# HGRN's tile products in seven visits a group instead of twelve, one block of three levels raised on VectorE

## What is computed

```
b = cumsum(log_f)                       # per chunk, per key channel
decay = exp(where(i >= j, b_i - b_j, -inf))
attn[i, j] = sum_k q[i,k] * decay[i,j,k] * k[j,k]
o_intra = attn @ v
o_off = (q * exp(b)) @ S_start          # state at the chunk's start
S = exp(b_last) * S + sum_j (k_j * exp(b_last - b_j)) v_j^T
```

## Time and profile before

| what | value |
|---|---|
| median of 3 runs | 3014.79 us |
| profiled execution, its own time | 3016.74 us |
| its span | 3015.0 us |
| granted TensorE clock over the span | 0.998 |
| TensorE busy | 2976.6 us (99%) |
| VectorE busy | 1751.1 us (58%) |
| ScalarE busy | 1351.2 us (45%) |
| GpSimd busy | 942.8 us (31%) |

### The profile page before, as it was taken

One profiled execution on the slowest core, in us unless ns is written; L12 is line 12 of the kernel. 1 busy time (PEld: TensorE's weight loads), 2 busy tenths in 40 slices (PEclk: granted clock), 3 DMA queues, 4 the chain that ended last, 5 costly groups with the idle time before them and its releaser, 6 DMA issues. The chain is left out here.

```text
span 3015.0 us, 57464 instructions
## 1 busy us (share of the span) xinstructions
PE 2976.6 (99%) x22229; PEld 2828.8 (94%) x22229; DVE 1751.1 (58%) x3002; ACT 1351.2 (45%) x2650; POOL 942.8 (31%) x1086
## 2 busy tenths in 40 slices
PE   6999999999999999999999999999999999999999
PEld 5899999999999999999999999999999999998887
DVE  4746857668568476685784633344368445455554
ACT  6445456455554554555645542212243222224443
POOL 0024435246245353462353520000113343340110
PEclk9999999999999999999999999999999999999999
DMA  7723122122122221221222325442311322227653
GB/s 259 266 65 102 52 78 80 49 78 82 45 91 71 61 96 49 79 78 49 73 82 65 121 91 155 137 127 84 125 39 53 87 65 75 77 65 247 201 182 104
DMA packets 294016, 300.29 MB, mean 100 GB/s; under 512 B 13240, under 2 KB 254768, under 8 KB 293808
## 3 DMA queue, kind: packets, MB, share of 16 engines
q1 hardware_dynamic: 247968, 230.17, 24.6%
q10 hardware_dynamic: 45840, 67.27, 7.1%
HBM read 247.93 MB, written 49.46 MB: 99 GB/s over the span
## 5 line engine op out<-in xcount | busy, mean ns | idle before, releaser
L889 PE MATMUL bank<-h_hi,w_hi 128*128 128x384 f32 x2496 | 863.7, 346 | 0.0
L889 PE MATMUL bank<-h_hi,w_lo 128*128 128x384 f32 x2496 | 836.0, 335 | 0.0
L889 PE MATMUL bank<-h_lo,w_hi 128*128 128x384 f32 x2496 | 835.2, 335 | 0.0
L889 PEld LDWEIGHTS bank<-h_hi,w_hi 128*128 128x128 f32 x2496 | 469.0, 188 | 12.7 <-issue 7.3
L889 PEld LDWEIGHTS bank<-h_lo,w_hi 128*128 128x128 f32 x2496 | 469.4, 188 | 0.6
L889 PEld LDWEIGHTS bank<-h_hi,w_lo 128*128 128x128 f32 x2496 | 468.6, 188 | 0.0
L2033 POOL TENSOR_TENSOR kq<-kq,fg 128x384 f32<-128x384 f32 x288 | 291.2, 1041 | 161.3 <-PE bank L1025 130.5
L1562 DVE SCALAR_TENSOR_TENSOR acc<-bank,taps,acc 128x372 f32<-128x372 f32 (+5 forms) x512 | 249.1, 507 | 68.0 <-ACT acc L1189 56.6
L1277 ACT ACTIVATE cumb<-cumb,tok_g 128x128 f32<-128x128 f32 x576 | 176.0, 389 | 72.7 <-POOL cumb L1994 72.7
L2439 PE MATMUL bank<-a_hi,v_hi 128*128 128x384 f32 x480 | 160.9, 335 | 2.7 <-DVEq L3227 1.9
L1530 DVE TENSOR_TENSOR w_lo<-raw,w_hi 128x1024 fp32r<-128x1024 f32 x104 | 140.3, 1349 | 38.3 <-ACT w_hi L1170 38.3
(11 more groups left out here) (389 smaller groups left out, 6897.2 us busy)
## 6 DMA issues: line engine op xcount, KB each, us to landing
raw<-in_w_in SPq DMA_DIRECT2D x104, 512.0 KB, 4.1
raw<-in_ffn_w SPq DMA_DIRECT2D x78, 512.0 KB, 5.7
cumb<-cum_scratch SPq DMA_DIRECT2D x72, 512.0 KB, 6.1
ada_late<-in_ada_w SPq DMA_DIRECT2D x8, 2048.0 KB, 9.4
raw_d<-in_ffn_w SPq DMA_DIRECT2D x32, 512.0 KB, 5.4
small<-gate_scratch ACTq DMA_DIRECT2D x72, 192.0 KB, 2.4
hid_scratch<-small SPq DMA_DIRECT2D x20, 576.0 KB, 3.6
s_sum<-hid_scratch ACTq DMA_DIRECT2D x53, 192.0 KB, 3.7
```

What stands on the lines that cost most here:

```text
L889: last = pe.matmul(out, w[i][:, k, :], h[:, k, blk(hb)], start=(k == 0 and j == 0), stop=(k == KT - 1 and j == 2))
```

## The change

Steps are made level by level, the three blocks one after the other, in seven visits (BURSTS). A visit's place is counted in k-steps of stage b: 16 is the end of unit 1, 26 lies inside unit 3 after two of its eight k-steps. Levels 0 and 1 share a visit. A third key buffer (a part of hs_f) lets each block have its own. VectorE raises block 0 of levels 1, 2 and 7 in slots 1, 3 and 11 (first_up), ahead of that slot's reading out of the bank; GpSimd raises the other 18. ScalarE's gathers get slots of their own: KA_EARLY ahead of that slot's tanh, KA_LATE between the tanh and the reading out. Merges, copies and joins are put in new slots.

```diff
-JOINS = {2: (1, 2), 4: (2, 3), 5: (3, 5), 6: (5, 8)}
+JOINS = {2: (1, 2), 3: (2, 3), 4: (3, 5), 6: (5, 8)}
+BURSTS = {16: (0, 1), 26: (2,), 36: (3,), 50: (4,), 64: (5,), 78: (6,), 92: (7,)}
+KA_EARLY = {1: [(1, 0), (1, 1), (1, 2)], 2: [(2, 0), (2, 1)], 3: [(2, 2), (3, 0), (3, 1)], 4: [(3, 2)], 5: [(4, 1)],
+            6: [(4, 2)], 7: [(5, 1)]}
+KA_LATE = {4: [(4, 0)], 6: [(5, 0)], 7: [(5, 2)]}
+FIRST_UP = {1: 1, 3: 2, 11: 7}
+UPS_DVE = [(lv, 0) for lv in FIRST_UP.values()]
+UPS_POOL = [(lv, b) for lv in range(1, LEVELS + 1) for b in range(NB) if (lv, b) not in UPS_DVE]
+MERGES = {2: (0, 1), 4: (2,), 5: (3,), 7: (4,), 9: (5,)}
+KEEPS = {10: [(6, 2)], 12: [(7, 1), (7, 2)]}
...
+        ka.append(hs_f[:, 3:6, :].rearrange("p c n -> p (c n)"))
...
+    def raised(eng, g, lv, b):
+        count, ups = (up_first, UPS_DVE) if (lv, b) in UPS_DVE else (up_ready, UPS_POOL)
+        eng.wait_ge(count.sem, count.at(g, ups.index((lv, b)) + 1))
...
                 for k in range(KT):
+                    if between is not None and k > 0:
+                        levels_at(g, KT * between + k)
                     for j, (w, h) in enumerate(((w_hi, h_hi), (w_hi, h_lo), (w_lo, h_hi))):
...
+            def levels_at(g, at):
+                for lv in BURSTS.get(at, ()):
+                    for b in range(NB):
+                        level_step(g, lv, b)
...
             def hgrn(g, k):
-                for i in steps_in(k):
-                    lv, b = level(i)
...
+                levels_at(g, KT * (k + 1))
...
+            def first_up(g, k):
+                if k not in FIRST_UP:
+                    return
+                lv = FIRST_UP[k]
+                wait(lv_ready, g, step(lv, 0) + 1)
+                if lv == 1:
+                    dve.wait_ge(q_ready, g * 3 + 3)
+                else:
+                    raised(dve, g, lv - 1, 0)
+                if lv in (2, 3, 4, 6):
+                    wait(decay_ok, g, {2: 1, 3: 2, 4: 3, 6: 4}[lv])
+                raise_level(dve, lv, 0).then_inc(up_first.sem, 1)
...
                     if k > 0 and (k - 1) // NB in CONV_TILES:
                         conv_silu(g, k - 1)
+                    first_up(g, k)
                     b_evac(g, k)
-                    if k in JOINS and k > 4:
+                    if k in JOINS and k >= 4:
                         join_decays(g, k)
```

More of the change, by code:

```diff
@@ L994, in turn_v @@
                 last.then_inc(v_turned, 1)
-            def hgrn(g, k):
-                for i in steps_in(k):
-                    lv, b = level(i)
[L1000 to L1031, removed]
@@ new lines, in levels_at, with level_step @@
+            def levels_at(g, at):
+                for lv in BURSTS.get(at, ()):
+                    for b in range(NB):
+                        level_step(g, lv, b)
+            def level_step(g, lv, b):
+                i = step(lv, b)
+                if lv == 0:
+                    pe.wait_ge(q_ready, g * 3 + 1)
+                elif lv <= IN_BLOCK:
+                    pe.wait_ge(ka_ready.sem, ka_ready.at(g, i - NB + 1))
+                else:
+                    raised(pe, g, lv - 1, b)
+                if b == 0:
+                    if lv == 1 or lv == 4:
+                        pe.wait_ge(ms_read, g * NB + (2 if lv == 1 else 3))
+                    elif lv == 3 or lv == 5:
+                        pe.wait_ge(v_kept, g * NB + (2 if lv == 3 else 3))
+                    elif lv > IN_BLOCK:
+                        pe.wait_ge(lv_merged.sem, lv_merged.at(g, 1 if lv == 6 else 5))
+                for j in range(CB):
+                    c = b * CB + j
+                    s = 1 << (lv - 1) if lv else 0
+                    w = max(BS, s)
+                    for t in range(P // w):
+                        rows = slice(w * t, w * (t + 1))
+                        out = lv_out(lv, b)[rows, j * w:(j + 1) * w]
+                        own = slice(c * P + w * t, c * P + w * (t + 1))
+                        other = slice(c * P + w * (t ^ 1), c * P + w * ((t ^ 1) + 1))
+                        if lv == 0:
+                            last = pe.matmul(out, k_sum[:, own], q_t[:, own], start=True, stop=True)
+                        elif lv <= IN_BLOCK:
+                            last = pe.matmul(out.rearrange("p (n two s) -> p n two s", two=2, s=s),
+                                             ka[b][:, j * P + w * t:j * P + w * (t + 1)],
+                                             pairs(1, 2, s, c * P + w * t, w), start=True, stop=True)
+                        else:
+                            last = pe.matmul(out, (kf_t, kb_t)[t % 2][:, own], (qf_t, qb_t)[t % 2][:, other],
+                                             start=True, stop=True)
+                last.then_inc(lv_ready.sem, 1)
@@ L1300, in ssd_rstd, with gather_keys, hgrn_late @@
                 act.activation(rstd, rstd, ACT.Exp, scale=-0.5).then_inc(rstd_ok, 1)
+            def gather_keys(g, lv, b):
+                if lv == 1:
+                    act.wait_ge(q_ready, g * 3 + 3)
+                else:
+                    raised(act, g, lv - 1, b)
+                s = 1 << (lv - 1)
+                act.activation(ka[b][:, :].rearrange("p (n two s) -> p n two s", two=2, s=s),
+                               pairs(0, 3, s, b * BW, BW), ACT.Copy).then_inc(ka_ready.sem, 1)
+            def hgrn_late(g, k):
+                for lv, b in KA_LATE.get(k, ()):
+                    gather_keys(g, lv, b)
             def hgrn(g, k):
@@ L1308, in hgrn @@
                                       ).then_inc(hs_loaded, 16)
[L1309 to L1325, removed]
+                for lv, b in KA_EARLY.get(k, ()):
+                    gather_keys(g, lv, b)
+                for lv, b in KEEPS.get(k, ()):
+                    wait(lv_ready, g, step(lv, b) + 1)
                     w = 1 << (lv - 1)
@@ L1688, in join_decays @@
                     wait(decay_ok, g, list(JOINS).index(k))
-                if k == 4:
-                    wait(up_ready, g, NB)
+                if k == 3:
+                    raised(dve, g, 1, 0)
+                    raised(dve, g, 1, NB - 1)
                 for lv in range(lo, hi):
@@ L1703, in hgrn @@
             def hgrn(g, k):
[L1704 to L1708, removed]
+                for lv in MERGES.get(k, ()):
+                    wait(lv_ready, g, step(lv, NB - 1) + 1)
                     out = at_in[:, :].rearrange("p (c i) -> p c i", i=BS)
@@ L2010, in ssd, with hgrn @@
                     sum_squares(g, 2)
[L2012 to L2019, removed]
+            def hgrn(g):
+                for lv, b in UPS_POOL:
+                    wait(lv_ready, g, step(lv, b) + 1)
                     if lv == 1:
                         pool.wait_ge(q_ready, g * 3 + 3)
[L2022 to L2034, removed]
+                    else:
+                        raised(pool, g, lv - 1, b)
+                    if lv in (2, 3, 4, 6):
+                        wait(decay_ok, g, {2: 1, 3: 2, 4: 3, 6: 4}[lv])
+                    raise_level(pool, lv, b).then_inc(up_ready.sem, 1)
             gather_taps(0)
@@ L2043, in _ @@
                     ssd(g, k)
[L2044 to L2048, removed]
+                wait(silu_done, g, 0)
+                gather_taps(g + 1)
+                hgrn(g)
                 for k in early:
@@ L2053, in _ @@
                 ssd(g, k)
-            for k in range(SLOTS):
-                hgrn(g, k)
+            hgrn(g)
 PHASES = [("s1", 4), ("s2", 4), ("h", 4), ("o", 4), ("up0", 2)]
```

34 lines of the change are left out of this document (24 added, 10 removed).

## The result

The changed kernel takes 3023.94 us, the median of 10 runs (3021.88 to 3026.45); the kernel before took 3015.77 in the same session (10 runs, 3013.10 to 3017.98). The ratio is 1.0027, with a 95% interval of 1.0018 to 1.0037: slower by 8.2 us. The profiled execution took 3025.2 us, its span 3023.4, at the same granted clock as before, 0.998.

The account below looks back on a forecast made before the run. TensorE, busy 99% of the span, was taken as the bound; 14.0 us saved on visits against new waits gave +7.0 us on the median 3014.79, so 3021.8 us, with 3003.5 to 3030 to hold 8 times in 10.

Parts of the forecast that it names:

- Fewer visits: TensorE, each group: 12 visits become 7 at 0.34 us each, plus 0.05 at slot 10; 14.0 us off over eight groups.
- A visit inside a unit costs as one at an edge: TensorE: a visit inside a unit adds nothing; if entering and leaving were paid a second time, 8 us more.
- VectorE's raises: VectorE takes turns with GpSimd for whole instructions: 1.5 us an instruction at level 1, 1.35 at level 2, 0.56 alone.
- Visit 3's third block: Level 3, groups 0 to 6: VectorE's chain and ScalarE's queue make gather (3,2) late; TensorE waits 1.6 us a group.
- Unit 11's bank: Groups 0 to 6: VectorE's queue frees the bank late for unit 11; a wait of 0.1 to 0.8 us, 0.7 taken.
- Smaller ones: Groups 0 to 6: visit 2's third block 0.25 us, banks of units 4 and 7 0.15 each; together 0.55 a group.
- Last group: Group 7, without taps: -1.75 us for visits, +1.05 for late gathers and third blocks; -0.7 in all.
- The sum: Whole kernel: +1.1 us in each of groups 0 to 6, -0.7 in the last; +7.0, slower by 0.23%.
- Rival A: All covers hold and TensorE keeps the 14.0 us: 3000.8 us; chance 0.14.
- B: Only one of the waits at visit 3 and unit 11 comes: 3010.6 or 3016.9 us; chance 0.25.
- C: VectorE's raises take 0.7 us an instruction and more: 3028; a visit inside a unit costing double: 3029.8; chance 0.13.
- D: The 0.34 us is paid per level or block change, not per visit, so nothing is won: 3036 us; chance 0.03.

Follow-up runs that it names:

- respaced_split: Against respaced: block 2's step of levels 2 to 6 made one k-step later, 12 visits a group again; 3013.52 us, 0.9995 of the kernel before.
- level1_apart: Against the changed kernel: GpSimd's first raise of level 1 waits until VectorE has raised block 0; 3025.55 us, 1.0031 of the kernel before.
- respaced: Against the changed kernel: visits 2 to 7 re-placed, gathers, merges and copies reordered, level 7's raise back on GpSimd; 3001.95 us, 0.9954 of the kernel before.
- visits_moved: Against the changed kernel: only the visits moved, to k-steps 16, 30, 41, 53, 67, 77, 89, other queues unchanged; 3029.12 us, 1.0046 of the kernel before.
- vector_raises_none: Against the changed kernel: VectorE raises nothing, GpSimd makes all 21 raises; 3036.22 us, 1.0069 of the kernel before.

## Why the prediction was right in its sign and where its sum was off

*Fewer visits* (forecast 14.0 us off). Measured: 13.3. Before, all the visits of a group cost 10.16 us with turn_v, after, without waits, 8.50: 1.66 a group instead of 1.75. The price per visit (0.34) was right to 0.01; five at 0.33 are 1.65, so of the 0.05 given to slot 10's mix nothing is left. respaced_split confirms it from the other side.

*A visit inside a unit costs as one at an edge* (priced at nothing). Right: 0.99 and 0.99.

*VectorE's raises* (1.5 us each at level 1, 1.35 at level 2). 3.02 and 2.68 for two: right, and for the reason given, as level1_apart shows (1.02 for two when alone). The Trainium skill, "SBUF — State Buffer", section "SBUF: two separate sides", calls the shared pair an exclusive lock, held for the whole instruction, and not a split of bandwidth. With that 3.02 against 1.02 agrees, where an even split would give 2.04. Two rows that the prediction put beside this say less than it took from them. The conv_silu of 0.56 at 536.63 was not free of raises, as shown above, and the rule does not say why it was short. The joins of 0.88 and 2.33 differ in size (576 and 1152 columns); the join of 1152 took 1.54 at 496.77 in the kernel before, also beside a raise.

*Visit 3's third block* (1.6, groups 0 to 6). 1.68, by the chain named. The arrival was forecast for 509.6 and came at 509.1, and TensorE wanted it at 507.5 instead of 508.0. Both are half a us early for one reason: group 1's stage b began at 484.86 in this execution and at 485.43 in that of before. The wait does not hang on it.

*Unit 11's bank* (0.1 to 0.8, 0.7 taken). This is the term that failed. It was 1.48 in groups 1 to 6 (1.21 in the view of waits). The count began with "record and middle tap 1.1, taps 3.03": it hid unit 7's conv_silu under the 1.1 of unit 8's middle tap, which holds for one of 0.56 and not for one of 1.29, and it let only the second one wait for GpSimd. Both were dear (1.29 and 1.25), the first at the end of level 5's raises, now one stretch of six instructions; the earlier trace rows had the first at 1.20 before too. And after a stop at a bank the second matmul starts 0.28 after the first instead of 0.173, as the earlier trace rows show it behind a visit (505.56, 505.85); the count had no such term at a bank. Together 0.8 x 7 = 5.5 us that the sum lacks. (The 10.1 us that the prediction gives for the kernel before run from the start of unit 9, 530.20 to 540.32; from the end of unit 8 there is a visit of 0.77 more. The term does not use them.)

*Smaller ones* (0.55 a group). 0.36 in group 1: visit 2 0.11, unit 6 0.17, unit 9 0.08, and not those that I named (units 4 and 7 were in time).

*Last group* (-0.7). -0.61: the waits came to the 1.05 that was forecast, the rest is in the visits.

*The sum.* +7.0 was forecast. With the measured terms: 7.0 + 0.7 (visits) + 5.5 (unit 11) + 0.6 (visit 3) - 1.3 (smaller ones) - 0.8 (group 0, whose unit 11 waited 0.4) - 0.7 (the wait of the earlier trace rows, in which the forecast saw no change) = 11.0, and the mixers show 10.9. The median says 8.2 (its interval reaches from 5.4 to 11.2), and 3023.94 lies within the range. That the median came out 2.1 us from the forecast is in part luck: the mixers were 3.9 us off, and 1.0 of the 2.1 is that before's own median was 3015.77 beside the changed kernel and 3014.79 in the three runs that the forecast was put on.

*Rival A* is what respaced shows: with all covers held seven visits, at other places, take 3001.95, forecast for that case 3000.8. *B*, that only one of the two large waits comes, is out: both came. *C* is out: alone a raise instruction of VectorE takes 0.51, not 0.7, and a visit inside a unit costs no more than at an edge. *D* (cost not per visit) is out by respaced_split. What stays open is why conv_silu under a raise takes 0.56 at one moment and 1.29 at another; and the share of the median's 8.2 us that is scatter of head and tail.

## What to carry to other kernels

When steps of a bound engine are gathered into fewer visits, count what the visit itself costs (here 0.33 us) and then, for each visit, whether its last piece of input is there when it is wanted: bursts make the other engines' work bursty too, and their lists have to be reordered with it. Repairing one late link shows the next one behind it, so move all the queues together (respaced), and read after each repair which wait took over. Look at the granted clock behind every longer stop of TensorE: it cost 1.2 to 2.7 us on top of a stop of 2.7 here.

## What the runs showed that I had not expected

The lower clock came around stops inside a stage of steady work: after 1.8 us in visits_moved (granted clock 0.52 in 3.4 us) and around a visit stretched by 2.7 us in vector_raises_none (0.50, starts 0.32 us apart). It did not come each time: the same stop brought it in four of the seven groups 0 to 6 of visits_moved and in six of the same seven of vector_raises_none. The stops of 1.5 us in the changed kernel were not followed by it.

A stop has a price of its own at the restart: after one at a bank, the second matmul starts 0.25 to 0.28 us after the first, where 0.173 would do; behind a visit it is 0.28 too.

Sharing raises between two engines that take turns still paid: VectorE lost 2 us at level 1 to the turns, and visit 2's third block came 2.5 us sooner than without its help.
